# Stores of the projections' results moved from SyncE's queue to GpSimd's in a two-layer encoder step

## What is computed

```python
p = rmsnorm(x) @ w_in[l]     # 1024 -> 3584: mixer a | b | c | cross-attention query | gate
# layer 0: attention over a band of chunks; layer 1: HGRN2 gated recurrence, for which
#   log_f = logaddexp(log(lb), log1p(-lb) + log_sigmoid(b));  k = (1 - lb) * sigmoid(-b)
y = concat(mixer_out, cross_attention_out) * silu(gate)
x = x + y @ w_out[l]
```

## Time and profile before

| | us |
|---|---|
| median of 3 runs | 2550.99 (2548.23 to 2551.62) |
| the profiled execution | 2550.28 |
| its span, first to last instruction | 2548.5 |

### The profile page before, as it was taken

One profiled execution on the slowest core, in us unless ns is written; L12 is line 12 of the kernel. 1 busy time (PEld: TensorE's weight loads), 2 busy tenths in 40 slices (PEclk: granted clock), 3 DMA queues, 4 the chain that ended last, 5 costly groups with the idle time before them and its releaser, 6 DMA issues. The chain is left out here.

```text
span 2548.5 us, 61164 instructions
## 1 busy us (share of the span) xinstructions
PE 2414.5 (95%) x23733; PEld 2129.7 (84%) x23733; DVE 1865.4 (73%) x3612; ACT 1457.2 (57%) x3336; POOL 359.8 (14%) x584
## 2 busy tenths in 40 slices
PE   6999999999979999999998899999999979999997
PEld 3899999999956777777776898999999967888886
DVE  5799788787655555555555899778787868888784
ACT  3464666665454555454554565676765646666663
POOL 1232000000012111111111233000000021211211
PEclk8999999999989999999999999999999999999999
DMA  5787887779893222222223788777778784344441
GB/s 178 242 288 253 275 277 253 233 232 295 249 282 113 62 80 80 61 78 61 84 76 140 237 276 267 252 251 241 236 251 279 264 257 137 117 132 126 131 132 65
DMA packets 402563, 480.61 MB, mean 189 GB/s; under 512 B 40516, under 2 KB 249212, under 8 KB 402280
## 3 DMA queue, kind: packets, MB, share of 16 engines
q1 hardware_dynamic: 385592, 416.51, 51.7%
q0 software_dynamic: 14848, 55.45, 6.3%
q10 hardware_dynamic: 1840, 4.75, 0.7%
HBM read 329.78 MB, written 151.56 MB: 189 GB/s over the span
## 5 line engine op out<-in xcount | busy, mean ns | idle before, releaser
L1388 PE MATMUL pj_acc<-x_hi,pj_wh 128*128 128x256 f32 (+1 forms) x3136 | 920.5, 294 | 39.9 <-DVE pj_wl L484 36.9
L1388 PE MATMUL pj_acc<-x_lo,pj_wh 128*128 128x256 f32 (+1 forms) x3136 | 907.8, 289 | 0.0
L1388 PE MATMUL pj_acc<-x_hi,pj_wl 128*128 128x256 f32 (+1 forms) x3136 | 907.7, 289 | 0.0
L477 ACT ACTIVATE pj_wh<-pj_wt 128x512 fp32r<-128x512 f32 x728 | 456.4, 634 | 365.7 <-DMA pj_wt<-tsum 276.4
L1388 PEld LDWEIGHTS pj_acc<-x_hi,pj_wh 128*128 128x128 f32 x3136 | 598.7, 191 | 56.2 <-DVE pj_wl L484 53.5
L484 DVE SCALAR_TENSOR_TENSOR pj_wl<-pj_wt,pj_wh 128x512 fp32r<-128x512 f32 x728 | 514.3, 720 | 122.1 <-ACT pj_wh L477 108.5
L1388 PEld LDWEIGHTS pj_acc<-x_hi,pj_wl 128*128 128x128 f32 x3136 | 599.0, 191 | 0.0
L1388 PEld LDWEIGHTS pj_acc<-x_lo,pj_wh 128*128 128x128 f32 x3136 | 598.5, 191 | 0.0
L1239 DVE TENSOR_TENSOR pj_out<-pj_out,pj_acc 128x512 f32<-128x512 f32 (+1 forms) x448 | 320.2, 715 | 82.0 <-PE pj_acc L1388 51.7
L2510 ACT COPY pb_pt<-pb_TP 128x384 f32<-128x384 f32 (+2 forms) x272 | 106.9, 393 | 300.7 <-PE pb_TP L2226 226.3
L2394 DVE COPY pb_pt<-pb_TP 128x256 f32<-128x256 f32 (+2 forms) x266 | 115.8, 435 | 143.1 <-PE pb_TP L2223 130.5
(11 more groups left out here) (340 smaller groups left out, 3870.3 us busy)
## 6 DMA issues: line engine op xcount, KB each, us to landing
pj_wt<-tsum SPq DMA_DIRECT2D x588, 256.0 KB, 3.7
proj<-pj_out SPq DMA_DIRECT2D x112, 512.0 KB, 4.1
tsum<-pj_wt SPq DMA_DIRECT2D x140, 256.0 KB, 3.2
pj_wraw<-in_w_in_dram POOLq DMA_DIRECT2D x24, 1024.0 KB, 6.2
tsum<-pj_wraw SPq DMA_DIRECT2D x56, 256.0 KB, 4.1
hg_x<-x_mid SPq DMA_DIRECT2D x17, 512.0 KB, 3.5
out_dram<-hg_x POOLq DMA_DIRECT2D x17, 512.0 KB, 3.0
pb_gate<-proj SPq DMA_DIRECT2D x16, 512.0 KB, 5.0
```

The lines of the kernel that those rows point to most:

```text
L477: nc.scalar.mul(self.hi[j][:], self.source(step), scale_of(c, self.l)).then_inc(self.s_hi, 1)
L1388: ins = nc.tensor.matmul(BANK[j][:, 0:n], a[j][:, k], x.of(y, p, j)[:, k], start=(k == 0 and i == 0), stop=(k == 3 and i == 2))
```

## The change

Both projections' `store` and `place_in` move from SyncE's program to GpSimd's, text unchanged but for the issuing engine. They stand at the end of GpSimd's iteration t, at the same t as before; GpSimd's loop gets 14 more iterations, so that the last stores are reached. The semaphores that the stores signal are now of the kind that DMAs issued by GpSimd use. What stays on SyncE are the fetches, the kept sums and the loads of the next stage. The number and the bytes of the DMAs are as before: in each layer 56 stores of `proj` with 28 small ones, in layer 1 also 12 of `kgate` with 6 small ones.

```diff
--- before.py
+++ after.py
@@ -226,7 +226,7 @@
         self.s_raw, self.s_val = ([sem(f"pb_{n}{i}") for i in range(3)] for n in ("raw", "val"))
         self.bias = far("pb_bias", [P, HA, BAND])
         self.s_big, self.s_sb = sem("pb_big"), sem("pb_sb")
-        self.s_st = [sem(f"pj0_st{i}") for i in range(2)]
+        self.s_st = [sem.software(f"pj0_st{i}") for i in range(2)]
 
     def blank(self, nc):
         nc.gpsimd.memset(self.bias[:, :, 0:self.SWIDE], BIG).then_inc(self.s_big, 1)
@@ -288,8 +288,8 @@
         self.s_ld, self.s_li, self.s_lx, self.s_lvals = (sem(f"sm_{n}") for n in ("ld", "li", "lx", "lvals"))
         self.s_lk = [sem(f"sm_lk{i}") for i in range(2)]
         self.s_q1, self.s_st, self.s_ca = (sem(f"sm_{n}") for n in ("q1", "st", "ca"))
-        self.s_store = [sem(f"pj1_st{i}") for i in range(2)]
-        self.s_store2 = sem("pj1_st2")
+        self.s_store = [sem.software(f"pj1_st{i}") for i in range(2)]
+        self.s_store2 = sem.software("pj1_st2")
 
     def two(self, a, width):
         return a.rearrange("p (n two m) -> p n two m", two=2, m=width)
@@ -1006,25 +1006,6 @@
         with nc.Block() as block:
             @block.sync
             def _(sp):
-                def store(q):
-                    p, c = divmod(q, WPAIRS)
-                    if kind_of(c) == plain:
-                        sp.wait_ge(s_cb, 4 * q + 4)
-                    else:
-                        sp.wait_ge(s_post, before(q) + 2 * each(q))
-                    groups = slice(2 * ORDER[c], 2 * ORDER[c] + 2)
-                    if kind_of(c) == forget:
-                        place_in(v["kgate"][groups.start - GK:groups.stop - GK], sig, p, s_st2)
-                    place_in(proj[groups], out[q % 2], p, s_st[q % 2])
-
-                def place_in(to, buf, p, s_done):
-                    sp.dma_start(to[:, :, 2 * HALF * p:2 * HALF * (p + 1)].rearrange("g p n -> p g n"),
-                                 buf[:, :, SHALF:SHALF + 2 * HALF]).then_inc(s_done, 16)
-                    if p == 0:
-                        for row in range(2):
-                            ends = bass.AP(buf[:].tensor, WIDE * row, [[2 * WIDE, P], [WIDE - SHALF, 2], [1, SHALF]])
-                            sp.dma_start(to[row, :, SEQ:NTOK].rearrange("p (h n) -> p h n", h=2), ends).then_inc(s_done, 16)
-
                 def load_sample(c, j):
                     tok = slice(SEQ, NTOK)
                     if (c, j) == (1, 2):
@@ -1074,10 +1055,6 @@
                     step = t - 3 + TERMS
                     if t >= 3 and step < STEPS:
                         w.keep(sp, step)
-                    if t >= 9 and (t - 9) % TERMS == 0 and pair(t - 9) < PASSES * WPAIRS and not each(pair(t - 9)):
-                        store(pair(t - 9))
-                    if t >= 11 and (t - 11) % TERMS == 0 and pair(t - 11) < PASSES * WPAIRS and each(pair(t - 11)):
-                        store(pair(t - 11))
                     if l and place(t)[0] == PASSES - 1:
                         load_sample(*place(t)[1:])
                     if not l and place(t)[0] == PASSES - 1:
@@ -1085,6 +1062,25 @@
 
             @block.gpsimd
             def _(pool):
+                def store(q):
+                    p, c = divmod(q, WPAIRS)
+                    if kind_of(c) == plain:
+                        pool.wait_ge(s_cb, 4 * q + 4)
+                    else:
+                        pool.wait_ge(s_post, before(q) + 2 * each(q))
+                    groups = slice(2 * ORDER[c], 2 * ORDER[c] + 2)
+                    if kind_of(c) == forget:
+                        place_in(v["kgate"][groups.start - GK:groups.stop - GK], sig, p, s_st2)
+                    place_in(proj[groups], out[q % 2], p, s_st[q % 2])
+
+                def place_in(to, buf, p, s_done):
+                    pool.dma_start(to[:, :, 2 * HALF * p:2 * HALF * (p + 1)].rearrange("g p n -> p g n"),
+                                 buf[:, :, SHALF:SHALF + 2 * HALF]).then_inc(s_done, 16)
+                    if p == 0:
+                        for row in range(2):
+                            ends = bass.AP(buf[:].tensor, WIDE * row, [[2 * WIDE, P], [WIDE - SHALF, 2], [1, SHALF]])
+                            pool.dma_start(to[row, :, SEQ:NTOK].rearrange("p (h n) -> p h n", h=2), ends).then_inc(s_done, 16)
+
                 def load_raw(c):
                     pool.wait_ge(w.s_dve, len(w.ON_DVE) * (c - 1))
                     pool.wait_ge(w.s_pool, len(w.ON_POOL) * (c - 1))
@@ -1102,7 +1098,7 @@
                     early.left(pool, v["s_stx"])
                 for j in w.ON_POOL:
                     w.add(nc, pool, j)
-                for t in range(ALL):
+                for t in range(ALL + 2 * TERMS):
                     step = t - 1 + TERMS
                     if t >= 1 and step < STEPS and step % TERMS in w.ON_POOL:
                         w.add(nc, pool, step)
@@ -1121,6 +1117,10 @@
                             i = 4 * p + c // 2
                             pool.wait_ge(s_ms, i + 1)
                             nc.gpsimd.tensor_tensor(rs[:, i:i + 1], ms[:, i:i + 1], neg_half[:, 0:1], ALU.pow).then_inc(s_rs, 1)
+                    if t >= 9 and (t - 9) % TERMS == 0 and pair(t - 9) < PASSES * WPAIRS and not each(pair(t - 9)):
+                        store(pair(t - 9))
+                    if t >= 11 and (t - 11) % TERMS == 0 and pair(t - 11) < PASSES * WPAIRS and each(pair(t - 11)):
+                        store(pair(t - 11))
 
             @block.scalar
             def _(act):
```

## The result

The changed kernel is slower: 2569.69 us (2564.1 to 2580.77, 6 runs) against 2547.94 us for the kernel before (2541.91 to 2551.62, 6 runs), ratio 1.0093 with a 95% interval of 1.0075 to 1.011, some 22 us more: under one per cent, but clear of noise. Its profiled execution took 2568.44 us, span 2566.7. In it the stores are L1077 (main) and L1082 (ends), now on GpSimd; L1134, L477, L484 and L1388 keep their numbers.

What follows compares the result with a forecast made beforehand. Fetches that feed TensorE were taken to stand behind stores' waits on SyncE, costing 14.3 us in layer 1's forget pairs. Terms -10 - 1.5 + 1 - 2 + 0.5 = -12 took 2551 to 2539 us; range 2528 to 2556.

Steps and rivals of the forecast that it cites:

- ceiling of 14.3 us: Layer 1's passes 1 to 3: time lost in forget stretches because weight fetches stand behind stores' waits; the most A could gain.
- A: Forget pairs, layer 1's passes 1 to 3: fetches go out on time once the store's wait leaves SyncE; -10 us, floor 4.
- what is late next: Step within A: VectorE's four extra steps and ScalarE's four sigmoids per forget pair keep some stall, so floor 4 us.
- B: Other stores of passes 1 to 3, both layers: issue and wait leave SyncE, mostly inside the slack; -1.5 us, 0 to -5.
- C: A store's issue on GpSimd: 0.6 us, bounds 0.53 and 1.08; hidden in passes 1 to 3, so 0.
- R4: Rival, pass 0's gate and forget pairs: each GpSimd issue waits for a VectorE step; +14 us, 2565 us, chance 0.05.
- D: Pass 0, plain and gate pairs: plain stores hidden, gate pairs' weight sums 0.1 us late; +1 us, -2 to +12.
- E: Pass 0, layer 1's forget pairs: weight sum 2.4 us later, kept sums sooner; -2 us, -6 to +6.6.
- R1: Rival, pass 0: GpSimd becomes late, deciding from about 1 us per issue; +7.6 us, 2559 us, chance 0.11.
- F: Ends of both blocks: GpSimd issues the last store, 0.6 for 0.37 us, with no loss in landing; +0.5 us.
- R2: Rival, forget pairs: load on VectorE and ScalarE replaces the store's wait; -4 us, 2547 us, chance 0.20.
- The signs named ahead: If right: no store waits on SyncE, layer 1's passes 1 to 3 about 434 us; if wrong: late sums, waits for proj.

Runs made afterwards that it cites:

- e8: Kernel before, all stores on SyncE, layer 1's forget pairs' stores in passes 1 to 3 two steps later in its order: 2543.66 us, ratio 0.9981.
- e9: Changed kernel with each layer's last store on SyncE and, in passes 1 to 3, the forget pairs' `proj` store ahead of `kgate`: 2553.74 us, ratio 1.0014.
- e1: Changed kernel, but the last pair's store of each layer is issued by SyncE: 2560.26 us, ratio 1.0052 to the kernel before.
- e4: Changed kernel, but the forget pairs' stores and the last one of each layer are issued by SyncE: 2553.95 us, ratio 1.0025 to the kernel before.
- e6: Kernel before with only pass 0's gate and forget pairs stored by GpSimd: 2552.51 us, ratio 1.001.
- e5: Kernel before with only pass 0's plain pairs stored by GpSimd: 2550.22 us, ratio 0.9999.
- e2: Kernel before, but the last pair's store of each layer is issued by GpSimd: 2562.7 us, ratio 1.0065.
- e12: Kernel before, all stores on SyncE, forget pairs' stores of passes 1 to 3 one step later, `proj` first: 2541.8 us, ratio 0.9977.
- e10: As e9, but all of pass 0's stores on SyncE too: 2541.37 us, ratio 0.9973 to the kernel before.
- e15: Kernel before with only layer 0's last store on GpSimd: 2557.44 us, ratio 1.0027.

## Why the prediction was wrong

Forecast 2539 us and faster; measured about 22 us slower than before, outside the range. Step by step:

- **What bounds the kernel: right in place and in size.** The forget pairs did lose time through SyncE's order (e8 wins 3.7 us in the stage by reordering alone). TensorE's waits in layer 1's passes 1 to 3 of the kernel before look smaller than the ceiling of 14.3 us:

```profile
PE pj_acc L1388 <- DVE pj_wl L484: 9.4, 19, 0.9
```

  But that counts idle time only. The matmuls start every 0.12 us, and around one of these waits they start so:

```profile
1706.07 0.28 PE L1388 MATMUL pj_acc<-x_lo,pj_wh 128*128 128x256 f32 x1
1706.74 0.39 PE L1388 MATMUL pj_acc<-x_hi,pj_wh 128*128 128x256 f32 x1 [0.39 <-DVE pj_wl L484]
1706.96 0.28 PE L1388 MATMUL pj_acc<-x_hi,pj_wl 128*128 128x256 f32 x1
```

  A wait of 0.39 us puts the next starts off by 0.55 and 0.10 us. Summed over the 19 waits that is 14.5 us. The ways above that gain leave 8 to 11 us of it, so the ceiling was there and most of it couldn't be had.

- **A, forget pairs, -10: wrong in sign; measured +4.1 with B in the stage (447.2 against 443.1).** The step that failed is "what is late next". It named ScalarE's sigmoids and VectorE's steps, and passed over ScalarE's first copy, which waits for the very store that was moved. "No reason for a loss" in the landing rested on a 3.0 us landing from a quieter stage; the stores landed in 4.7 us by the median, and the forget pairs' `proj`, second of two, 4.6 to 6.6 us after its issue. e9 shows that this wait took the gain. The size of -10 was wrong too: the best kernels gain 4 to 6 us there. It leaned on 8.4 us between the layers, but the window of layer 1 in the earlier trace rows begins in pass 0 (17 matmuls more than layer 0's); by the table it is 443.1 against 437.2, 5.9 us.
- **B, other stores, -1.5: not seen.** Layer 0's passes 1 to 3, which have only such stores, take 437.8 us against 437.2 (435.5 in e1), and e4, which moves these stores and not the forget pairs', takes the 443.1 us of before in layer 1's.
- **C, the price of an issue, 0.6 us: 0.73, inside the bounds.** The issues of `proj` (ns min/median/max, first and last start us), none of them near R4's price:

```profile
L1077 POOL DMA_DIRECT2D proj<-pj_out x112: 707/727/758, 93.9 to 2059.6; - x112
```

  In passes 1 to 3 they hide, as forecast.
- **D and E, pass 0, together -1: measured +5.2 in layer 1, -0.2 in layer 0.** The mechanism is R1's: GpSimd late with its weight sums. D saw it at the price of 0.6 us and let the late sum go as "not at once needed"; E took the sum's lateness as harmless because the kept sum would go out sooner. Neither asked who else reads the sum: ScalarE's high part, and behind it VectorE and TensorE (e6). R1 set its point of decision near 1 us per issue; it came at 0.73, since three issues stand ahead of the sum. D's "hidden too" for a plain pair's landing was wrong as well: GpSimd issued it late behind the raw weights' load, and ScalarE waited (e5), though at small cost.
- **F, the two ends, +0.5: measured +9.9 in the gaps alone, and 0.0065 of the time when nothing else is changed (e2).** With A's (14 us and more in the stage) this is the largest miss. Neither makes the whole loss: without the ends the change is still at 1.0052 (e1). F weighed the issue of the last store (0.6 for 0.37 us) and not what an end of a block waits for. Before, the next stage started 1.6 us after the issue of SyncE's last store with the transfer under way; that this holds for GpSimd was assumed, and no row showed it. What the runs show in its place: GpSimd's DRAIN at the end of the block, hidden before because GpSimd was done 200 us early, became the last thing in the block, 4.3 to 5.9 us from the issue on.
- **R2**, the wait replaced by another on ScalarE, was the right kind but for the wrong reason (load, not landing), and ended at a gain. **R4**, the lock between GpSimd and VectorE, did not come, but was hardly put to the test: the issues lie between 707 and 758 ns, yet none of them ran beside L1251, L1252 or L1328. Two loads of raw weights ran beside L1252 after the change and took 0.91 us, as elsewhere. The rule in the Trainium skill ("SBUF — State Buffer", section "SBUF: two separate sides") speaks of VectorE's two-port modes alone; no run here shows which steps use them, and so it is neither borne out nor refuted.
- The signs named ahead did their work: SyncE's waits lost their store lines, issues were short, sums in pass 0 were late after gates, ScalarE waited for `proj`. The fall to 434 us didn't come. And the range named as reaching "up to most of R1" ended at 2556, below R1's 2559.

## What to carry to other kernels

When a DMA is moved to another queue, follow its landing as well as its issue: the next writer of its buffer is the one who waits, and of two stores the one whose buffer is needed first goes first. Before giving GpSimd a store, look at what GpSimd does last before the end of a block, and count the small DMAs that it would issue ahead of its own arithmetic. And where a fetch stands behind a store's wait, try the order within the queue first: one step later and `proj` first brought 0.9977 of the time with no queue changed (e12), as much as the best split over two queues (e10, 0.9973).

## What the runs showed of the hardware

- With the last store of a block on GpSimd's queue, all engines stood until 5.3 to 7.0 us after its issue (e2: 694.26 to 699.60; after: 695.42 to 702.37), 4 us of them without a byte moving in layer 0 of the changed kernel; with the store on SyncE the next stage began 1.6 us after the issue. GpSimd runs one DRAIN in that time. Counted with the last operation, it took 2.6 us with no transfer of GpSimd's under way (before, 1835.7; 1.7 to 4.0 in the other kernels whose GpSimd ends the block so), 4.3 to 5.9 with the block's last store; SyncE's took 0.12 us behind one.
- A store of 512 KB took 4.7 us to land from GpSimd, 4.1 from SyncE, by the median of each kernel. The last store of a block, with nothing else moving, took 3.2 us from GpSimd and 2.7 from SyncE. The Trainium skill ("DMA: Bandwidth & Descriptors", section "Latency and other measured facts") gives a first byte after about 1 us by GpSimd and 0.6 by SyncE; the sign agrees.
- At an end with GpSimd's store the granted clock falls, and for longer than at the others. All engines in two stretches (us, busy of PE, PEld, DVE, ACT, POOL, then PEclk, DMA share, GB/s), of before and then of after:

```profile
696.00:704.00 8.00, 5.58 (x55) 4.16 (x54) 4.68 (x10) 2.36 (x5) 0.00 (x0) 1.00 0.69 216
704.00:720.00 16.00, 12.83 (x156) 9.10 (x155) 6.78 (x21) 8.42 (x19) 1.38 (x4) 0.79 0.90 257
```

```profile
696.00:704.00 8.00, 1.63 (x8) 1.66 (x9) 0.76 (x3) 0.51 (x1) 0.14 (x1) 0.60 0.20 74
704.00:720.00 16.00, 12.88 (x115) 9.09 (x114) 7.67 (x18) 7.80 (x17) 0.74 (x2) 0.77 0.89 253
```

  Before, TensorE stood for 2.4 us and the clock stayed at its upper level (1.00, 2.4 GHz) to 707 us. After, TensorE stood for 8.0 us and the clock was at its lower level (0.50, 1.2 GHz) from 697.6 to 707.8 us, 5.4 us of that behind the gap. At all five ends with GpSimd's store it was low for 6.8 us or more; at the 27 others it was low for 3.4 us around the gap or stayed up through it. The first three transposes behind the gap take 0.87 us, where four took 0.63 before. In the time of the stage behind layer 0's gap this hardly shows: 705.3 us after the change, 707.3 in e2 and e15, 701.4 to 706.5 in the kernels with the short gap.
